# Loads into 128 partitions by one DMA, and four-fold heads stored by residue

## What is computed

```python
B_PAIRS = ((128, 1), (512, 4), (2048, 16))
B_HEADS = 4

def dilated_mixer(q, k, v, slopes):
    n, T, _, H, hd = q.shape
    outs, lses = [], []
    for p, (w, r) in enumerate(B_PAIRS):
        def fold(a):
            return a.reshape(n, T // r, r, H, hd).transpose(0, 2, 1, 3, 4).reshape(n * r, T // r, H, hd)
        o, lse = banded_attention(fold(q[:, :, p])[:, :, :, None], fold(k[:, :, p]), fold(v[:, :, p]),
                                  w // r, slopes[p * H:(p + 1) * H].reshape(H, 1), r)
        outs.append(o.reshape(n, r, T // r, H, hd).transpose(0, 2, 1, 3, 4).reshape(n, T, H, hd))
        lses.append(lse.reshape(n, r, T // r, H).transpose(0, 2, 1, 3).reshape(n, T, H))
    alpha = jax.nn.softmax(jnp.stack(lses, axis=0), axis=0)
    o = jnp.einsum('pnth,pnthd->nthd', alpha, jnp.stack(outs, axis=0).astype(jnp.float32))
    return o.reshape(n, T, H * hd)

def reference(x, ..., w_down):
    ...
        h = rmsnorm(x, g_mix_pre[l])
        z = h @ w_in[l]
        (aq, akc, avc, aks, avs, akw, avw, agate,
         bq, bk, bv, cq, ck, cv) = jnp.split(z, list(IN_SPLITS), axis=-1)
        o_a = nsa_mixer(...)
        o_b = dilated_mixer(bq.reshape(bshape), bk.reshape(bshape), bv.reshape(bshape), sl_b)
        o_c, _ = banded_attention(...)
        mix = jnp.concatenate([o_a, o_b, o_c], axis=-1) @ w_out[l]
        x = x + rmsnorm(mix, g_mix_post[l])
        f = conv_glu_ffn(rmsnorm(x, g_ffn_pre[l]), w_up[l], conv_w[l], conv_b[l], w_down[l])
        x = x + rmsnorm(f, g_ffn_post[l])
    return x
```

## Time and profile before

| What | us |
|---|---|
| Time, median of 3 runs | 3173.92 |
| Lowest and highest | 3173.43, 3177.03 |
| Span of the profiled execution | 3174.1 |
| Projection | 0 to 688.6 |
| Compression | 688.6 to 722.9 |
| Attention, k, b units | 722.9 to 1013.9 |
| Attention, c units | 1013.9 to 1103.2 |
| Attention, w and s units | 1103.2 to 1590 |
| Output projection and feed-forward | 1590 to 3174.1 |

### The profile page before, as it was taken

One profiled execution on the slowest core, in us unless ns is written; L12 is line 12 of the kernel. 1 busy time (PEld: TensorE's weight loads), 2 busy tenths in 40 slices (PEclk: granted clock), 3 DMA queues, 4 the chain that ended last, 5 costly groups with the idle time before them and its releaser, 6 DMA issues. The chain is left out here.

```text
span 3174.1 us, 44910 instructions
## 1 busy us (share of the span) xinstructions
PE 3066.0 (97%) x16138; PEld 2501.5 (79%) x16138; DVE 2058.5 (65%) x3930; ACT 1472.0 (46%) x2657; POOL 1211.7 (38%) x845
## 2 busy tenths in 40 slices
PE   8999999998998999999989989999999999999998
PEld 8888888887776776666668878888888788888887
DVE  5565566556767987777744587777645577777443
ACT  5332533236666866665633444444434344444332
POOL 2444254310000024442110098888210698885010
PEclk9999999998999999999999999999999999999999
DMA  4465555378778743332234522222565222223553
GB/s 141 161 186 149 169 162 174 114 209 195 183 187 215 175 114 73 96 99 50 84 93 132 162 99 80 87 80 80 175 200 201 102 85 80 93 80 110 182 199 106
DMA packets 262540, 425.58 MB, mean 134 GB/s; under 512 B 126801, under 2 KB 162897, under 8 KB 250321
## 3 DMA queue, kind: packets, MB, share of 16 engines
q1 hardware_dynamic: 252752, 385.28, 41.4%
q0 software_dynamic: 9568, 37.43, 3.7%
HBM read 304.19 MB, written 126.84 MB: 136 GB/s over the span
## 5 line engine op out<-in xcount | busy, mean ns | idle before, releaser
L1080 PE MATMUL z_banks<-ops,z_area 128*128 128x512 f32 x1720 | 434.1, 391 | 3.2 <-DVE z_area L834 3.2
L3153 PE MATMUL f_banks<-f_wt 128*128 128x512 f32 x1776 | 406.1, 389 | 0.0
L3153 PEld LDWEIGHTS f_banks<-f_wt 128*128 128x128 f32 x1776 | 333.3, 188 | 69.2
L1080 PEld LDWEIGHTS z_banks<-ops,z_area 128*128 128x128 f32 x1720 | 323.0, 188 | 70.4 <-DVE z_area L834 3.6
L2540 POOL TENSOR_TENSOR f_wt<-f_wt_f,f_wt 128x1024 fp32r<-128x1024 f32 x132 | 320.2, 2449 | 60.3 <-ACT f_wt L2668 59.4
L2022 ACT ACTIVATE w_small<-w_small,a_stats 128x128 f32<-128x128 f32 (+3 forms) x510 | 257.3, 517 | 110.7 <-DVE a_stats L2108 82.6
L3124 PE MATMUL f_banks<-low,f_wt 128*128 128x512 f32 x704 | 275.3, 391 | 0.0
L2108 DVE CUSTOM_DVE_ANT_0 w_small<-a_s_ps,near 128x128 f32<-128x128 f32 (+2 forms) x456 | 166.2, 392 | 110.1 <-PE a_s_ps L1908 86.8
L2949 DVE SCALAR_TENSOR_TENSOR near<-w_small,vk,near 128x1024 f32<-128x1024 f32 x88 | 232.3, 2640 | 1.7
L3124 PE MATMUL f_banks<-f_oo,f_wt 128*128 128x512 f32 x704 | 218.0, 391 | 3.2 <-issue 3.0
L1952 PE MATMUL a_ot_ps<-a_turned_w,vs 128*64 128x256 f32 (+3 forms) x1452 | 220.9, 427 | 0.0
(11 more groups left out here) (305 smaller groups left out, 7120.4 us busy)
## 6 DMA issues: line engine op xcount, KB each, us to landing
f_wt_f<-in_w_ffn SPq DMA_DIRECT2D x74, 512.0 KB, 4.1
z_area_f<-in_w_z SPq DMA_DIRECT2D x54, 512.0 KB, 5.1
low<-z_hi SPq DMA_DIRECT2D x48, 512.0 KB, 7.9
f_raw_f<-in_w_ffn SPq DMA_DIRECT2D x22, 1024.0 KB, 4.8
f_wt_f<-in_w_ffn SPq DMA_DIRECT2D x22, 1024.0 KB, 5.3
g_up<-near SPq DMA_DIRECT2D x44, 512.0 KB, 2.6
f_wt_f<-g_up SPq DMA_DIRECT2D x88, 256.0 KB, 4.4
low<-z_lo SPq DMA_DIRECT2D x39, 512.0 KB, 8.6
```

Source lines behind the costliest of these rows:

```text
L1080: last = pe.matmul(banks[:, bank, :], w[:, c * P:(c + 1) * P], rows[:, c * 512:(c + 1) * 512], start=(first and c == 0 and q == 0), stop=( ...
L3153: last = pe.matmul(banks[:, 2 * t + n, :], g[:, tok], w[:, n, :], start=(d == 0 and x == 0), stop=(d == NF - 1 and x == 2))
```

## The change

Four things change. `z_hi` and `z_lo` become the two halves of one DRAM tensor, `z_parts` [2, 33*128, 2048]. The two DMAs of a query load become one, whose source has the dimensions 2 x 64 x 2048 and whose destination is 128 partitions of 2048; the two DMAs of the upper keys become one, whose source walks the same 64 rows twice (a dimension of 2 with step 0); the eight of the windows become four, with sources of 2 x 64 x 1024. The third load of the keys (lower part, 64 rows) stays. The two pairs of blocks of fold-4 heads get a new kind, "quarter": ACT and DVE read the bank with a step of four and write the residues apart, and the stores go out in runs of 512 bytes. In `scores` all operands are neighbouring columns then.

```diff
-PAIRS = (..., ("split", 3, 4),
-         ("split", 5, 6), ("wide", 26, 27), ("split", 12, 13), ("four", 24, 25), ("folded", 7, 8), ("split", 14, 15),
-         ("split", 16, 17))
+PAIRS = (..., ("split", 3, 4),
+         ("quarter", 5, 6), ("wide", 26, 27), ("split", 12, 13), ("four", 24, 25), ("folded", 7, 8), ("split", 14, 15),
+         ("quarter", 16, 17))
...
 def load_windows(eng, z_pair, x_raw, x_in, m):
     for g in range(2):
-        for odd in range(2):
-            eng.dma_start(x_raw[odd * HD:(odd + 1) * HD, m, g, :],
-                          z_pair[m, odd, g * HD:(g + 1) * HD, :]).then_inc(x_in[m], 16)
+        eng.dma_start(x_raw[:, m, g, :], z_pair[m, :, g * HD:(g + 1) * HD, :]).then_inc(x_in[m], 16)
+
+def both_parts(z_parts, row):
+    return z_parts[:, row:row + HD, :]
+
+def upper_twice(z_parts, row):
+    return z_parts[0, row:row + HD, :].unsqueeze(0).to_broadcast([2, HD, T])
...
+                if kind == "quarter":
+                    for z, slot in ((z_hi, hi_slot(s)), (z_lo, lo_slot(s))):
+                        dst = z[rows, :].rearrange("p (r l) -> p r l", r=4)[:, :, tile * P:(tile + 1) * P]
+                        sp.dma_start(dst, quarter_slot(slot).bitcast(F32)).then_inc(stored[s], 16)
+                    return
...
+                elif kind == "quarter":
+                    act.activation(quarter_slot(hi_slot(0)), by_quarter(bank), ACT.Copy).then_inc(zhi_done, 1)
...
+                elif kind == "quarter":
+                    out, bank = quarter_slot(out), by_quarter(bank)
+                    left = out if s == 3 else by_quarter(left)
                 dve.tensor_tensor(out, bank, left, ALU.add).then_inc(done, 1)
...
             def load_q(n, u):
-                rows, s = slice(units[u].q_row, units[u].q_row + HD), q_at.slot[n]
-                sp.dma_start(q2[0:HD, s, :].bitcast(F32), z_hi[rows, :]).then_inc(q_in[s], 16)
-                sp.dma_start(q2[HD:P, s, :].bitcast(F32), z_lo[rows, :]).then_inc(q_in[s], 16)
+                s = q_at.slot[n]
+                sp.dma_start(q2[:, s, :].bitcast(F32), both_parts(z_parts, units[u].q_row)).then_inc(q_in[s], 16)
...
             def load_k(n, u):
-                for half in range(2):
-                    sp.dma_start(k_hi[s][half * HD:(half + 1) * HD, :].bitcast(F32), z_hi[rows, :]).then_inc(k_in[s], 16)
-                sp.dma_start(k_lo[s][0:HD, :].bitcast(F32), z_lo[rows, :]).then_inc(k_in[s], 16)
+                sp.dma_start(k_hi[s].bitcast(F32), upper_twice(z_parts, units[u].k_row)).then_inc(k_in[s], 16)
+                sp.dma_start(k_lo[s][0:HD, :].bitcast(F32), z_parts[1, rows, :]).then_inc(k_in[s], 16)
...
-                tok = "p (b j r) -> p r b j"
-                query = q2[:, qs, :].rearrange(tok, r=unit.fold, j=P)[:, res, b, :]
-                if unit.fold == NT:
-                    query = q2[:, qs, res * P:(res + 1) * P]
+                query = q2[:, qs, t * P:(t + 1) * P]
...
-                    hi = k_hi[ks].rearrange("p (l r) -> p r l", r=unit.fold)[:, res, :]
-                    lo = k_lo[ks].rearrange("p (l r) -> p r l", r=unit.fold)[:, res, :]
-                    if unit.fold == NT:
-                        hi, lo = (k[:, res * P:(res + 1) * P] for k in (k_hi[ks], k_lo[ks]))
+                    hi, lo = (k[:, res * per * P:(res + 1) * per * P] for k in (k_hi[ks], k_lo[ks]))
```

More of the change, by code:

```diff
@@ L105, in split_total @@
 def split_total(g):
-    return sum({"split": 4, "folded": 4, "single": 2}.get(kind_of(i), 0) for i in range(g))
+    return sum({"split": 4, "folded": 4, "quarter": 4, "single": 2}.get(kind_of(i), 0) for i in range(g))
 def lower_total(g):
-    return sum({"split": 3, "folded": 3, "single": 1}.get(kind_of(i), 0) for i in range(g))
+    return sum({"split": 3, "folded": 3, "quarter": 3, "single": 1}.get(kind_of(i), 0) for i in range(g))
 def turn_total(g):
@@ L122, in stores_before @@
     per = {"split": (32, 32, 32, 32), "plain": (32, 32, 32, 32), "four": (32, 32, 32, 32), "wide": (64, 64, 64, 64),
-           "folded": (32, 0, 32, 0), "single": (32, 32, 0, 0)}
+           "folded": (32, 0, 32, 0), "quarter": (32, 32, 32, 32), "single": (32, 32, 0, 0)}
     return sum(per[kind_of(i)][slot] for i in range(g))
@@ L209, in lo_slot, with by_quarter, quarter_slot @@
             return st_lo[:, s, :]
+        def by_quarter(tile):
+            return tile.rearrange("p (l r) -> p r l", r=4)
+        def quarter_slot(tile):
+            return tile.rearrange("p (r l) -> p r l", r=4)
         def folded(tile):
@@ L613, in upper_z @@
                 kind = kind_of(g)
-                if kind not in ("split", "folded", "single") or kind == "single" and s > 1:
+                if kind not in ("split", "folded", "quarter", "single") or kind == "single" and s > 1:
                     return
@@ L854, in lower_z @@
                     src = folded(banks[:, 0, :]) if s == 0 else lo.bitcast(F32)
+                elif kind == "quarter" and s == 0:
+                    hi, lo, src = quarter_slot(hi), quarter_slot(lo), by_quarter(src)
                 dve.tensor_tensor(lo, src, hi.bitcast(F32), ALU.subtract).then_inc(zlo_done if s else a_free, 1)
@@ L868, in add_p7 @@
                     out, bank, left = folded_slot(st_lo, 3).bitcast(F32), folded(bank), folded(e)
+                elif kind_of(g) == "quarter":
+                    out, bank, left = quarter_slot(out), by_quarter(bank), by_quarter(left)
                 dve.tensor_tensor(out, bank, left, ALU.add).then_inc(e3_done, 1)
@@ L1161, in compress @@
 def compress(nc, z_pair, w1_copy, b1_t, w2, overlap, x_raw, w_raw, w_hi, poss, x_in, w_in, pos_in, last_out, keys_in, kc_hi, kc_lo, vk, idt,
-             z_hi, z_lo, bias_b, cmp_bias, low, near):
+             z_parts, bias_b, cmp_bias, low, near):
     U = T // 2
@@ L1225, in _ @@
             for s, unit in enumerate(first[:2]):
-                rows = slice(unit.q_row, unit.q_row + HD)
-                sp.dma_start(low[0:HD, s, :].bitcast(F32), z_hi[rows, :]).then_inc(units_in, 16)
-                sp.dma_start(low[HD:P, s, :].bitcast(F32), z_lo[rows, :]).then_inc(units_in, 16)
+                sp.dma_start(low[:, s, :].bitcast(F32), both_parts(z_parts, unit.q_row)).then_inc(units_in, 16)
             sp.dma_start(near[:, 0, 0:CW], cmp_bias[0]).then_inc(units_in, 16)
@@ L1234, in _ @@
                 sp.dma_start(vk[:, g, HD + 1:], overlap).then_inc(over_in, 16)
-            for half in range(2):
-                sp.dma_start(low[half * HD:(half + 1) * HD, 2, :].bitcast(F32), z_hi[rows, :]).then_inc(keys_in, 16)
-            sp.dma_start(low[0:HD, 3, :].bitcast(F32), z_lo[rows, :]).then_inc(keys_in, 16)
+            sp.dma_start(low[:, 2, :].bitcast(F32), upper_twice(z_parts, first[2].k_row)).then_inc(keys_in, 16)
+            sp.dma_start(low[0:HD, 3, :].bitcast(F32), z_parts[1, rows, :]).then_inc(keys_in, 16)
             sp.wait_ge(over_in, 16 * G)
             sp.wait_ge(last_out, 4 * 16)
-            sp.wait_ge(units_in, 16 * 6)
+            sp.wait_ge(units_in, 16 * 4)
         @blk.gpsimd
@@ L1669, in attend @@
         for n, s in enumerate(kv_at.slot):
-            k_seen[s] += 48 if n != 1 else 0
+            k_seen[s] += 32 if n != 1 else 0
             k_count.append(k_seen[s])
@@ L1686, in load_qm @@
                 sp.wait_ge(sel_out[units[u].h // R], 64)
-                sp.dma_start(qm[0:HD, :].bitcast(F32), z_hi[rows, :]).then_inc(qm_in, 16)
+                sp.dma_start(qm[0:HD, :].bitcast(F32), z_parts[0, rows, :]).then_inc(qm_in, 16)
                 sp.dma_start(qm[HD:HD + NS, :].bitcast(F32), sel_t[units[u].h // R]).then_inc(qm_in, 16)
@@ L3270, in layer @@
             compress(nc, z_pair, w1_copy, b1_t, w2, overlap, x_raw, w1_raw, w1_hi, poss, x2_in, w1_in, pos_in, last_out, keys_in,
[L3271 removed]
+                     kc_hi, kc_lo, vk, idt, z_parts, bias_b, cmp_bias, low, near)
         w_in = keep.enter_context(nc.semaphore("w_out_in"))
```

15 lines of the change are left out of this document (7 added, 8 removed).

## The result

The changed kernel takes 3809.9 us (median of 4 runs, 3808.0 to 3811.1), the kernel before 3173.7 in the same comparison (4 runs, 3173.0 to 3177.0). The ratio is 1.200 with a 95% interval of 1.199 to 1.202: 636 us slower. The profiled execution has a span of 3808.3. The forecast was 3725 in a range of 3600 to 3880.

The account below looks back on a forecast made before the run. PE, busy 97% of the span, bounded the kernel; after the change two DMA engines would set the pace. 3174.1 + 530 (to the first w unit) + 21 (w and s units) = 3725 us, range 3600 to 3880.

Parts of the forecast that it names:

- two engines: Merged loads, source outermost dimension 2: only two DMA engines work, 20.2 us per 1 MiB; chance 0.85 at full pace.
- both sides must be cut at the same places: Merged loads: destination and source are cut alike, only at the outermost dimension; the reason for taking 20.2 us per MiB.
- rival 1: Merged loads: all 16 engines work, 2.5 us per load, kernel faster at 3145 us (3135 to 3165); chance 0.10.
- Rival 2: Merged loads: two engines, each held at 16 GB/s, 32.8 us per load, total 4280 us; chance 0.03.
- SP's issuing isn't on the path, so this is worth nothing: Merged loads: SP issues one DMA less for queries and one less for keys, charged 0 us.
- The middle: The k, b and c units: two engines never without work and set the time, +480 us.
- The w and s units: Units after the c units: loads hidden again, except 16 us at the first s unit and 5 at the group change.
- The weight of an engine's pace: Whole forecast: one GB/s more or less of an engine moves the total by 22 us.
- The strided score matmuls: Fold-4 score tiles: removing the step of four columns saves about 0.3 us in each of 64, 19 us of PE.
- it is worth that as long as PE sets the pace: Fold-4 score tiles: caveat that the 19 us count only where PE sets the pace, and nothing elsewhere.
- The new stores and copies: Projection, four pairs taken out with a step of four: 0 to 6.4 us of DVE, 1 us taken.
- the waits for the table: DVE's waits for the table behind queries and keys, 9.1 us: with all 16 engines they shrink by half or go.

Follow-up runs that it names:

- after_table_first: The changed kernel with the bias table issued ahead of the next queries and keys instead of behind them: 3818.0 us, beside the changed kernel's 3809.9.

## Why the prediction was right, and where it was short

**The mechanism was right.** The step "two engines" rested on where a DMA can be cut, an argument from the shapes that no row of the kernel before could decide. Its first half, that single pieces go to different engines, was taken from one time of 3.5 us, which says only that more than two engines worked. The trace of the kernel before has more: the first load of `w_copy`, issued at 145.19 us, is 16 packets of 16 KB, all 16 of them under way at once and landed by 148.24. No DMA there has an outermost dimension under 16 in its destination (1077 DMAs: 16, 32, 64, 128 or 2048), and each has 16 landings. Its second half is shown by the share of 0.13 and the sweep over 2, 4 and 128 pieces. That both sides must be cut at the same places is shown only so far: 128 partitions on the side of the destination didn't help a source of 2 pieces. And rival 1 came true, 8 us above its number and inside its range, once the source had 128 rows. Rival 2 (two engines at 16 GB/s each) is excluded by the 53 GB/s, 26.5 for each of the two. Why loads into 64 partitions run at 16 GB/s per engine, no run takes apart.

**The terms.** Between the spans the forecast was short by 83 us: 12 ahead of the attention, 36 in the k, b and c units, 35 behind them. All three parts were short, so the total isn't right by errors that cancel.

- *"SP's issuing isn't on the path, so this is worth nothing"* is the step that failed for the start. It holds for the kernel before, where the issue of a load of keys took 0.6 us (median). Here SP stood for 25.76 us at the windows and 13.09 at a small load behind the second weight:

```profile
681.61 25.76 SPq L79 DMA_DIRECT2D ops<-z_pair  x2
707.42 9.13 SPq L400 DMA_DIRECT2D z_parts<-z_st_hi  x1
...
722.08 13.09 SPq L1248 DMA_DIRECT2D c_b1s<-in_b_t  x1
735.22 2.67 SPq L1250 DMA_DIRECT2D c_kw<-in_w  x2
737.94 0.47 SPq L1251 DMA_DIRECT2D c_vw<-in_w  x1
738.45 2.23 SPq L1255 DMA_DIRECT2D low<-z_parts  x2
```

  The queries of the first units were issued at 738.5, behind a second weight that was in only at 740.9, as ACT's wait for it shows:

```profile
740.92 3.90 ACT L1333 ACTIVATE ops<-ops 128x1024 fp32r<-128x1024 f32 x4 [3.56 <-DMA ops<-w_copy]
```

  The sum had them begin at 728.6. The 12.3 us between are the whole miss of the start (784.9 for 772.5). The run with merged windows alone shows SP's standing by itself: its total was forecast to a microsecond, the start of its attention to two.
- *The middle.* The two busy engines never stop there: from 784.9 to 1681.0 two or more packets are under way in 99.8% of the time, exactly two in 76%. So what was missed isn't in pauses but in what the engines carry. The merged loads came out slightly cheaper (19.8 for 20.2, 14 us less over 36 of them), so some 50 us are in the small DMAs, whose shares of a sixteenth pass through the two busy engines: in the sum 1.3 for lower keys and values, 0.4 for a table and 2 for a result. Two stretches of the changed kernel, between two merged loads and at a load of lower keys:

```profile
896.00:902.00 6.00, 1.69 (x8) 1.35 (x10) 1.55 (x10) 1.71 (x5) 0.00 (x0) 0.50 0.13 43
...
918.00:922.00 4.00, 0.00 (x0) 0.00 (x0) 0.00 (x0) 0.00 (x0) 0.00 (x0) 0.50 0.65 156
```

  In the first the two engines are busy (0.13) but move 43 GB/s; in the second, 0.65 of 16 engines move 156 GB/s, 15 GB/s per engine, which is the pace of 64 partitions in the earlier trace rows, not the 25.9 at which I had charged the lower keys. That is one us for each of 13. A load of values took each engine eight packets of 229 ns (mean of the packets of 4160 bytes from 784 to 1681 us), 1.8 us where I had 1.3. The rest of the 50 I can't divide among tables, results and what the sum left out. That it isn't the table's place in the queue is shown by `after_table_first`. A triple took 117.6 us where the forecast had 111, but not as 22 + 45 + 45: it was 46.8 + 46.7 + 24.2. SP's order tells why: the table of the k unit stands behind a load of queries and the keys of the b unit after it, that of the first b unit behind two merged loads as well, that of the second behind one.
- *The w and s units.* I charged 5 us at the change of the group. It cost 23.7 (61.73 us for a unit of 38.07). The wait is that of DVE for `a_far`, from the view of who waits for this tile:

```profile
its engine sat idle before it (us, times) until:
...
  DMA a_far<-in_bias_s: 24.6, 1
```

  This load of 1 MiB is needed in the same unit and stands behind a merged load of queries and one of keys, 39.6 us on two engines. I had counted what the merged loads delay of themselves, and not this DMA behind them. At the first w unit, whose successor's keys come late, 29 us were lost (55.19 for 26.03) where I had 16.
- *The weight of an engine's pace* was worked out too small, though the sum doesn't use it: the sum has 42 times 20.2 us of merged loads (two windows of 512 KB counted as one), so one GB/s of 25.9 moves it by some 33 us, not 22. The range holds either way.

**The strided score matmuls.** The pace was right (0.64 to about 0.35 us a tile) and PE lost 3.7 us a unit, near the 4.8 charged. That "it is worth that as long as PE sets the pace" was the caveat that decided: in the two units with rows above, the time fell by about half of what PE lost. The gain by itself is 6 us, not 18. This would also explain why the run with 128 rows gave 3152.7 and not rival 1's 3145; I haven't taken that difference apart.

**The new stores and copies.** 1 us was taken; in the profile of storage alone the attention starts 1.7 us later.

**The loads of 64 partitions.** By rival 1 the waits for the table would go with merged loads on 16 engines. They do: unit 4 takes 15.1 us with 128 rows, 18.35 before. But the table ahead of the loads has the same effect (15.1) with loads as slow as before. So either remedy is enough, and faster loads aren't needed for it.

## What to carry to other kernels

Look at the outermost dimension of a DMA's source (the side that was varied here) before merging two into one: a source of 2 x 64 rows, or one row range walked twice, ran on two engines here and took 19.8 us per MiB, and 128 neighbouring rows ran on sixteen (share 0.99). In the trace it shows as a DMA share near the number of pieces over 16 (0.13 for 2, 0.25 for 4) while everybody waits. When one engine's share of a queue becomes long, charge three things to it: its bytes, the sixteenth of every other DMA behind it (some of which are needed sooner; a table's last landing came 26 to 44 us after its issue here), and the issuing engine itself, which stood (25.8 us at the windows) and came late to its next wait. And where an arithmetic engine waits for a small transfer, look first at what stands ahead of it on the queue.

## What the runs showed of the hardware

- With loads into 128 partitions a DMA engine moved 26.5 GB/s when only one other worked beside it, and 25.9 when all 16 did (53 and 415 GB/s in all). For these loads the pace of one engine hardly depended on the others; for loads into 64 partitions it was 16 with all 16 at work (266 GB/s at a share of 1.04), and 15 at a share of 0.65 (156 GB/s).
- SP's issue of one load of keys took 0.6 us before (median of L1693 and of L1694). In the changed kernel the issue of lower keys behind two merged loads took 31.1 us (L1718, at 887.9), and the two issues of windows 25.8; the instructions behind them on SP wait as well (the table behind those lower keys was issued at 919.07).
- The cost of three kinds of slow loads was not additive: 691 us one by one, 642 together.
